# First attention of a hybrid decoder layer on one Trainium2 core: steps of three units, and VectorE copying the small unit's transposed block

## The reference, cut to what matters

```
fox:  s = q k^T / 8 + cum[t] - cum[s];  p = softmax(causal s);  o = p v          (6 heads of 64)
pool: trailing means minus the token, mapped per group, scaled                    (256 wide)
nsa:  o = g0 * softmax(s_c) v_c + g1 * softmax(s_s) v_s + g2 * softmax(s_w) v_w   (6 heads, 2 kv heads)
x = x + concat(fox, pool, nsa) @ w_out
```

## Time and profile before

| | |
|---|---|
| median of three runs | 804.26 us |
| profiled execution, span from first to last instruction | 801.5 us |
| PE busy, share of the span | 95% |
| DVE, ACT, POOL | 67%, 58%, 22% |
| chain that ended last | PE 89%, DVE 5%, ACT 2% |
| mean granted TensorE clock | 0.992 |

### The profile page before, as it was taken

How to read it: one execution, slowest core, us unless ns; L and a number is a source line. 1 busy time by engine, 2 the same in 40 slices (tenths; PEclk the granted TensorE clock), 3 DMA queues, 4 the chain that set the end, 5 groups by cost and what they waited for, 6 DMA issues and landing times.

```text
span 801.5 us, 11865 instructions
## 1 busy us (share of the span) xinstructions
PE 760.8 (95%) x4204; PEld 587.0 (73%) x4204; DVE 535.5 (67%) x742; ACT 462.7 (58%) x704; POOL 178.8 (22%) x185
## 2 busy tenths in 40 slices
PE   3999999989999999999999988999999999999994
PEld 3978789756767889888798873577777777777763
DVE  4535378577776435532354278588999888989986
ACT  4445662476776315632353062478778788777862
POOL 2900022000000102000000010124555544455412
PEclk9999999999999999999999998999999999999998
DMA  9834521000042534553101658999999999999962
GB/s 294 212 106 126 163 82 58 1 2 1 2 159 89 173 107 133 187 179 105 54 1 53 258 240 329 342 388 375 386 386 380 371 375 374 369 384 384 382 216 105
DMA packets 61903, 166.90 MB, mean 208 GB/s; under 512 B 8224, under 2 KB 36192, under 8 KB 49576
## 3 DMA queue, kind: packets, MB, share of 16 engines
q1 hardware_dynamic: 56376, 150.69, 50.9%
q0 software_dynamic: 4480, 12.48, 6.5%
q10 hardware_dynamic: 1008, 3.21, 1.1%
HBM read 153.44 MB, written 12.85 MB: 207 GB/s over the span
## 4 chain that ended last, share of the span: by engine, by line
PE 89%; DVE 5%; ACT 2%; issue 1%; DMA 1%; POOL 0%; POOLq 0%; ACTq 0%; DVEq 0%
PE ps L1863 23%; PE ps L1865 22%; PE ps L1864 22%; PE ps L2051 2%; PE ps L2134 2%; PE ps L2116 2%; PE ps L2268 2%; PE ps L2083 2%; PE ps L1980 2%; DVE nmax L1563 1%; PE ps L2087 1%; PE ps L2248 1%; PE ps L2190 1%; PE ps L2090 1%; DVE tok L1322 1%
## 5 line engine op out<-in xcount | busy, mean ns | idle before, releaser
L1302 DVE TENSOR_TENSOR wlo<-raw,whi 128x2048 fp32r<-128x2048 f32 x30 | 68.7, 2290 | 93.4 <-ACT whi L872 93.3
L1863 PE MATMUL ps<-whi,mhi 128*96 128x512 f32 (+1 forms) x276 | 109.4, 396 | 2.0 <-DVE mlo L1795 1.2
L1865 PE MATMUL ps<-whi,mlo 128*96 128x512 f32 (+1 forms) x276 | 108.9, 394 | 0.0
L1864 PE MATMUL ps<-wlo,mhi 128*96 128x512 f32 (+1 forms) x276 | 108.2, 392 | 0.0
L1310 DVE TENSOR_TENSOR wlo<-arena,whi 128x2048 fp32r<-128x2048 f32 x39 | 89.3, 2290 | 18.8 <-ACT whi L885 18.8
L728 POOL TENSOR_SCALAR stat<-stat 128x1 f32<-128x1 f32 x18 | 11.5, 640 | 375.3 <-ACT tok L891 225.9
L872 ACT ACTIVATE whi<-raw 128x2048 fp32r<-128x2048 f32 x30 | 57.3, 1910 | 57.0 <-PE ps L1865 56.9
L885 ACT ACTIVATE whi<-arena 128x2048 fp32r<-128x2048 f32 x39 | 74.7, 1915 | 24.8 <-PE ps L1865 24.8
L1863 PE MATMUL ps<-ahi,whi 128*128 128x512 f32 x192 | 75.9, 395 | 0.0
L1863 PE MATMUL ps<-whi,ahi 128*128 128x512 f32 (+1 forms) x192 | 70.9, 369 | 4.8 <-DVE wlo L1302 4.8
L1865 PE MATMUL ps<-ahi,wlo 128*128 128x512 f32 x192 | 74.9, 390 | 0.0
(11 more groups left out here) (374 smaller groups left out, 1697.5 us busy)
## 6 DMA issues: line engine op xcount, KB each, us to landing
arena<-in_exp_w_gate SPq DMA_DIRECT2D x30, 1024.0 KB, 16.6
arena<-in_exp_w_up SPq DMA_DIRECT2D x17, 1024.0 KB, 15.9
raw_a<-in_exp_w_down SPq DMA_DIRECT2D x16, 1024.0 KB, 18.3
raw<-in_exp_w_up SPq DMA_DIRECT2D x15, 1024.0 KB, 15.5
arena<-in_exp_w_down SPq DMA_DIRECT2D x9, 1024.0 KB, 20.7
raw<-in_exp_w_down SPq DMA_DIRECT2D x7, 1024.0 KB, 17.1
raw<-in_w_in SPq DMA_DIRECT2D x5, 1024.0 KB, 6.3
raw<-in_w_in SPq DMA_DIRECT2D x10, 512.0 KB, 5.3
```

Of the source, the lines that this page charges most:

```text
L1302: v.tensor_tensor(wlo[:, n % SPLIT, :], raw[:, n % RAW, :], whi[:, n % SPLIT, :].bitcast(F32), ALU.subtract).then_inc(lo_done, 1)
L1863: mm(out_, ahi_, bhi_, start=first, stop=False)
L1864: mm(out_, ahi_, blo_, start=False, stop=False)
L1865: return mm(out_, alo_, bhi_, start=False, stop=last)
```

## The change

The first attention gets functions of its own on PE, ACT and DVE; the second one keeps the old loop, with the same instructions. The first now goes in 18 steps of three units (`Triples`): two units are one head each of the large tile (3, later 2), the third is both heads of the small tile (0, later 1), side by side in one PSUM bank. Steps are three fox pairs, then s, w for each of three NSA pairs, for tiles 3 and 0, and the same for tiles 2 and 1.

- PE in step j: the scores of step j (three banks), the transposes of step j - 1 (now three banks, 3 to 5), the value products of step j - 2 (bank 6 for the large tile, 7 for the small one). The compressed transposes go together, four in one bank, after step 2's and step 11's.
- ACT: the exponentials of step j, the copies of the two large units of step j - 1 (and the one copy of the compressed block), the high parts of step j - 2.
- DVE: three maxima of step j (the small tile's two heads by one instruction), then their reciprocals and scalings, then **the copy of the small unit's transposed block of step j - 1**, which ACT made before, then the low parts of step j - 2.
- `win` takes banks 3 and 4. The scores of step 0 come between its two groups on PE, the pool mixer's copies right after step 0, and the window values' transposes after the transposes of step 0.
- The first tile of `out0` (tile 3) comes before the value products of the last step, its other tiles after. `out0` waits for the last exponentials and, in bank 3, for the last copies. The banks of the later dense groups are shifted by two.

The loops over the steps come first, of PE, ACT and DVE in this order, then the functions that they call on PE and DVE.

```
+            for j in range(1, PA.n):
+                scores(j)
+                transposes(j - 1)
+                if j == 1:
+                    window_transposes()
+                else:
+                    values(j - 2)
+            transposes(PA.n - 1)
+            values(PA.n - 2)
+            dense(KEY["out0"], TILES_A[0:1])
+            values(PA.n - 1)
+            dense(KEY["out0"], TILES_A[1:])
...
+            for j in range(1, PA.n):
+                exps(j)
+                copies(j - 1)
+                if j == 1:
+                    act.wait_ge(vw_tp, 1)
+                    a.activation(Vw[:, :, :], ps[6][:, :].rearrange("p (t n) -> p t n", t=NT), ACT.Copy).then_inc(vwT_done, 1)
+                else:
+                    outs_hi(j - 2)
...
+            for j in range(1, PA.n):
+                maxes(j)
+                scales(j)
+                small_copy(j - 1)
+                if j >= 2:
+                    outs_lo(j - 2)
...
+            def scores(j):
+
+                for u, i, kind, heads, nb in PA.three_of(j):
+                    bank, qc = ps[u % 3], slice(i * P, (i + 1) * P)
+                    if u >= 3:
+                        pe.wait_ge(PA.exp_done, u - 2)
...
+            def transposes(j):
+
+                for u, i, kind, heads, nb in PA.three_of(j):
+                    t = PA.turned(u)
+                    if t >= 3:
+                        PA.copied(pe, t - 3)
...
+                    pe.wait_ge(PA.scaled, u + 1)
+                    for b in range(nb * len(heads)):
+                        ins = nc.tensor.transpose(ps[3 + t % 3][:, P * b:P * (b + 1)], Pr[u % len(Pr)][:, P * b:P * (b + 1)],
+                                                  ident[:, :])
+                    ins.then_inc(PA.tp_done, 1)
...
+            def maxes(j):
+
+                for u, i, kind, heads, nb in PA.three_of(j):
+                    n, c = len(heads), PA.col(u)
+                    dve.wait_ge(PA.scores_done, u + 1)
+                    v.tensor_reduce(nmax[:, c:c + n], ps[u % 3][:, 0:P * nb * n].rearrange("p (e k) -> p e k", e=n), AX.X, ALU.max,
+                                    negate=True).then_inc(PA.max_done, 1)
...
+            def small_copy(j):
+
+                u, i, kind, heads, nb = PA.three_of(j)[2]
+                t, w = PA.turned(u), P * nb * len(heads)
+                dve.wait_ge(PA.tp_done, t + 1)
+                if j >= 2:
+                    dve.wait_ge(PA.pv_done, 2 * (j - 2) + 2)
+                v.tensor_copy(PTr[u % len(PTr)][:, 0:w], ps[3 + t % 3][:, 0:w]).then_inc(PA.small_pt, 1)
```

More of the change, by code:

```diff
@@ L367, in evacs, with __init__ @@
             return sum(x[5] == eng for x in groups[:g + 1])
[L371 to L375, removed]
         UX = [(i, "x", h, MT) for i in range(NT) for h in range(MEM_H)]
         LAG_T, LAG_V = 3, 5
[L381 to L393, removed]
+        class Signals:
+            def __init__(self, name):
                 self.scores_done = sem(name + "_scores_done")
@@ L418, in job @@
                 u = k - LAG_V
[L419 to L427, removed]
+                return u if self.has(u) else None
             def tile_outs(self, t):
[L431 to L433 removed]
+                return MEM_H * (t + 1)
             def bank(self, q):
                 return ps[5 + q % 3]
[L439 to L440 removed]
             def has(self, u):
@@ L1041, in mixed_hi @@
                 a.activation(ahi[:, 3 + f, :], ps[6 + f][:, :], ACT.Copy, scale=pscale[:, f, :]).then_inc(mix_hi, 1)
-            for n in range(4, KEY["out0"]):
+            for n in range(4, KEY["win"]):
                 key = ORDER[n]
@@ L1083, in attention, with outs_hi @@
+            def outs_hi(j):
+                if PA.kinds[j] != "s":
+                    tiles, f = PA.spot[j]
+                    for b, i in enumerate(tiles):
+                        act.wait_ge(PA.pv_done, 2 * j + b + 1)
+                        a.activation(ahi[:, f, i * P:(i + 1) * P], ps[6 + b][:, 0:P], ACT.Copy).then_inc(PA.o_hi, 1)
             def attention(ph, k0=0, k1=None):
                 for k in range(k0, ph.steps if k1 is None else k1):
-                    if ph.score(k):
-                        s = ph.sidx[k]
+                    if ph.has(k):
@@ L2019, in _ @@
             ins.then_inc(cum_mm, 1)
-            for n in range(5, KEY["out0"]):
+            for n in range(5, KEY["win"]):
                 dense(n)
@@ L2093, in attention @@
-                        ins.then_inc(ph.scores_done, 1)
-                    if ph is PA and k == LAG_T:
-                        first_transposes()
-                    if ph is PA:
-                        transpose(ph, k - LAG_T)
-                    j = ph.job(k)
-                    if j is not None:
-                        q, first, last = ph.out_of(j)
-                        u = k - LAG_V
+                        for e in range(2):
+                            ins = mm(bank[:, 0:MEM], QTx[:, 2 * h + e, qc], KTm[:, 2 * h + e, :],
+                                     start=(e == 0), stop=(e == 1))
@@ L2136, in attention @@
+                        if u >= 3:
+                            pe.wait_ge(ph.o_lo, u - 2)
+                        pt = PTr[u % len(PTr)]
+                        for f in range(2):
+                            for b in range(nb):
+                                c0 = 2 * P * h + P * f
+                                ins = mm(bank[:, P * f:P * (f + 1)], Vm[:, b, c0:c0 + P], pt[:, P * b:P * (b + 1)],
+                                         start=(b == 0), stop=(b == nb - 1))
                         ins.then_inc(ph.pv_done, 1)
+            dense(KEY["win"], (0,))
@@ L2139, in _ @@
             pe.wait_ge(evac["act"], evacs(of_piece[KEY["fv1"]][-1], "act"))
             pe.wait_ge(cumrow_in, 32)
-            attention(PA)
-            dense(KEY["out0"])
+            scores(0)
+            dense(KEY["win"], (1,))
+            for j in range(1, PA.n):
[3 more added lines that the diff above has]
+                    window_transposes()
+                else:
+                    values(j - 2)
+            transposes(PA.n - 1)
+            values(PA.n - 2)
```

360 lines of the change are left out of this document (219 added, 141 removed).

## The result

The changed kernel takes 796.38 us (median of 4 runs, 795.78 to 797.20) where the kernel before took 804.02 beside it (4 runs): ratio 0.9900, 95% interval 0.9888 to 0.9912, so 7.6 us faster. The forecast was 792.7, 11.3 us fewer than these 804.02 (11.6 by its own reckoning). The profiled execution has a span of 795.1 us, at a mean granted clock of 0.986.

What follows compares the result with a forecast made beforehand. PE, busy 95% of the span, was taken as the bound. Phase: 85.85 of steps + 0.5 start + 0.6 end = about 87.0 against 98.63 us, 11.6 less; 804.26 - 11.6 = 792.7, range 789.3 to 799.5.

Steps and rivals of the forecast that it cites:

- The steps of PE: First attention on PE: fox steps 5.05 us, NSA pairs 9.13 in tiles (3, 0), 8.85 in (2, 1); sum 85.85.
- The price of standing apart: PE's value groups: 0.24 us each for passage and fixed part, paid once when a step's two are neighbours.
- Rival 1: Value groups side by side on PE keep their fixed 0.14 us: 2.5 us more, 795.2; chance 0.20.
- Scores behind scores: PE's scores following scores instead of alternating with transposes: priced at zero, bounds plus and minus 0.1 us at 36 places.
- Rival 5: Scores behind scores on PE "lose 0.1" at each of 36 places: 789.1; chance 0.07.
- The compressed transposes: Eight on PE, with four of the window values, at 0.11 us each plus three passages of 0.10: 1.6 us.
- The clock: Granted in full in each stretch of the old profile, so durations were taken to need no correction.
- Start and end: PE's losses at the first attention's ends: 0.5 us at the start (bounds 0 and 1.9), 0.6 at the end (0 and 1.6).
- DVE at nothing: DVE busy 8.6 of PE's 8.85 us per NSA pair in tiles (2, 1), yet priced at nothing through the step's slack.
- Rival 2: DVE sets the pace in NSA, pairs of 10.1 and 9.6 us: 5.2 us more, 797.9; chance 0.23.
- Rivals 3 and 4: 3: DVE's strict order makes steps 5.8 us, 812.7, chance 0.05. 4: gain given back before the experts, 804.3, chance 0.04.

Runs made afterwards that it cites:

- mid_act: `cmp_both` with ACT's copy of the compressed block ahead of the small unit's exponential and the small unit's copy on ACT instead of DVE: 791.32 us, ratio 0.9838.
- both_late0: `cmp_both` with step 0's scores put behind the second `win` group again, as in the kernel before: 794.45 us, ratio 0.9871.
- both_tail: `cmp_both` with the last value groups ahead of all of `out0`, as in the kernel before: 792.13 us, ratio 0.9841.
- both_twice: `cmp_both` with DVE making the copy of the small unit's transposed block twice: 798.94 us, ratio 0.9928.
- both_mid: `cmp_both` with ACT's copy of the compressed block moved ahead of the small unit's exponential: 792.56 us, ratio 0.9847.
- cmp_both: Changed kernel with both halves' compressed transposes moved from the ring of three banks to bank 7, one step later behind the scores: 793.06 us, ratio 0.9855.
- after_act: Changed kernel with the copy of the small unit's transposed block back on ACT, the steps of three kept: 795.69 us, ratio 0.9893.
- both_act: `cmp_both` with the copy of the small unit's transposed block on ACT instead of DVE: 792.04 us, ratio 0.9841.
- cmp_second: Changed kernel with only the second half's compressed transposes moved to bank 7: 795.82 us, ratio 0.9894.
- cmp_first: Changed kernel with only the first half's compressed transposes moved to bank 7: 793.49 us, ratio 0.9866.

## Why the prediction was right, and where it was not

The sign, the range and, for most of the gain, the mechanism were right; a third of the forecast gain did not come. The time lies in the range because the range was made wide for other rivals, not because this loss was foreseen. By the forecast's steps:

- **The steps of PE.** Right. `mid_act`, whose PE never waits, gives by the same measure as above (with the 2.96 us from `out0`'s start to the last values, as in the changed kernel) 92.66 - 2.96 + 1.25 - 5.58 = 85.37 us, against the sum of 85.85. Fox steps came at 5.08 for 5.05, NSA pairs at 8.74 for 8.85 and 8.98 (182.43 to 191.41) for 9.13.
- **The price of standing apart,** 0.24 a step from two rows, with two neighbours paying it once: 0.27 measured. Rival 1 is out.
- **Scores behind scores** at zero: nothing to the contrary, since the steps come at their sum. Rival 5 is out; its 789.1 is the time if each such place were 0.1 shorter, though its words, "lose 0.1", say the opposite (0.1 longer would be 796.3), and it lies just below the stated range.
- **The compressed transposes.** This is the step that failed. The forecast put them at "1.6" together with the window values, as so many instructions at 0.11 and three passages, and stopped there. It did not ask which bank they take and who must have emptied it. In the old order the compressed units were small units among others; in the new one they are a fourth turn in a ring of three, and so wait for a copy of their own step, that ACT makes behind four exponentials. What is queued ahead of the awaited instruction was asked of DVE, not here. Price: 1.94 + 1.46 us of idle time.
- **The clock.** The forecast took it as full because it was full before. From 171.73 to 176.97 are 5.24 us; the same compressed transposes (0.57 at 217.50), value group (1.24 at 211.82) and scores of a (3, 0) step (1.84 in the changed kernel, 184.12 to 185.96) are 3.65. So 1.59 us, lost behind the idle time.
- **Start and end.** 0.5 and 0.6 forecast, nothing and 0.26 measured. `both_late0` shows the 1.4 that the early scores save. The reason given for the end was wrong, as `both_tail` shows.
- **DVE at nothing.** Right by a hair. 8.6 us a pair were forecast, 8.52 of 8.74 are busy, and, in `both_twice`, 1.37 us more work in a pair made the last one 1.53 longer. Rival 2 is out for this kernel, but its cause took back part of `both_mid`'s gain.
- **Rivals 3 and 4** are out: apart from the two steps with the compressed wait none takes 5.8 us, and 7.66 us of the phase are 7.6 in the time. What the forecast says against rival 4, that PE is busy without a gap after 253.92, isn't so: it waits 4.99 us ahead of the router. That wait came along with the stage, 5.00 us in the changed kernel.

The sum as measured: 85.37 + 0.26 + 3.40 + 1.59 = 90.62 of 90.97 us. The 0.35 left is not assigned. Taken together, the terms of the two waits and the clock are borne out by `cmp_both`: 1.42 (1.94 less 0.52), 1.06 and 1.59 are 4.07, and its stage is 4.01 shorter. With the two waits the forecast's sum would have been 792.7 + 3.4 = 796.1, and with the clock 797.7; the other terms were 1.3 too high together (0.48 in the steps, 0.84 at start and end), which hid part of the miss.

The Trainium skill, VectorE: DVE Perf Modes, section Specifications, puts ScalarE closer to PSUM and VectorE closer to SBUF. The traces agree in the direction: a 512-column copy out of PSUM is 0.684 us on DVE and 0.613 on ACT. The kernels with the copy on ACT are no slower (`after_act`, `both_act`), and where DVE's lateness set the end it was better there, by the trace (`mid_act` against `both_mid`).

## To carry to other kernels

When work is regrouped into larger turns of a ring, go through the turns that don't fit the pattern: for each, write down whose bank it takes, who empties it and what that engine has queued ahead. A pattern with a step of slack has none at an odd turn. Instructions of one tile shape belong side by side on PE, and an idle time of two microseconds, in one piece or in two close together, may cost nearly as much again in the clock. And an engine that just keeps up hides nothing: what is won on PE comes back as a wait at the first place where PE's own work doesn't stretch, here the last transposes.

## Hardware not expected

In the changed stage the granted clock fell behind three idle times of PE of 1.94, 1.95 and 2.17 us at 170 to 172 us (the changed kernel, `cmp_second`, `after_act`), to 0.54, 0.50 and 0.50 in the window 174:176, and was 1.00 again by 176 to 178 or 178 to 180. It stayed at 1.00 behind idle times of 1.46, 1.55 and 1.45 us at 215 to 218 (the changed kernel, `after_act`, `cmp_first`), and of 1.23 at 162 (`both_late0`). The length of a single idle time doesn't decide it alone: in `both_twice` it fell to 0.50 (window 244:246) behind two shorter ones, 1.12 and 0.98 us with 0.94 us of work between them, and cost 1.6 us. What else decides these runs don't tell, and it wasn't tried by itself.
